# Moving operands in rows of 528 elements and token halves of 256 and 264 in a two-layer hybrid decoder step

## The chip, the cores and the metric

The kernel runs on one core of a Trainium2 chip. The metric is the time of one execution on the device in microseconds (us); lower is better. Times of runs are given as the median of several executions; where a profile is read, it is one execution taken by the hardware profiler.

## The reference: what is computed

One inference step of a decoder with two layers, for a prompt of 512 tokens and 8 sample tokens, 1,024 features wide, all in float32. Layer 0 is a Mamba-2 (SSD) mixer, layer 1 a gated short convolution; each starts with an RMS norm and ends with a residual add, and a last RMS norm follows. Cut to what matters here:

```python
h = rmsnorm(x, norm_w[0])
proj = h @ w_in                         # 1024 -> 5152: z (2048), x/B/C (3072), dt (32)
xBC = silu(causal_dwconv(xBC) + conv_b)
y, state = ssd_chunked(xs, dt, A, B, C, ssm_state)
y = grouped_rmsnorm((y + D * xs) * silu(z), norm_w, 4)
x = x + y @ w_out                       # 2048 -> 1024

h = rmsnorm(x, norm_w[1])
bg, cg, xin, z = split(h @ sc_w_in)     # 1024 -> 4 x 2048
x = x + (bg * causal_dwconv(cg * xin) * silu(z)) @ sc_w_out
y = rmsnorm(x, final_norm_w)
```

Nearly all of the arithmetic is in the four products with weight matrices: `ssd_w_in`, `ssd_w_out`, `sc_w_in`, `sc_w_out`.

## The kernel before, in words

Activations lie transposed in SBUF: features on the 128 partitions, the 520 tokens (512 prompt and 8 sample, `T`) along the free dimension. The 1,024 features of a layer's input are `KT` = 8 rows of 520 tokens (`hhi[:, k, :]`), the 2,048 features that go into an output projection are 16 rows.

**Three products for one.** To keep float32 accuracy at the rate of the rounded type fp32r, weights and activations are split into a rounded high part and a low remainder: `whi`, `wlo` for the weights (ScalarE's `high`, L527, rounds a chunk of 128x1024; VectorE's `low`, L1065, subtracts), `hhi`, `hlo` for the inputs, `yhi`, `ylo` for what enters an output projection. A product is then whi·hhi + whi·hlo + wlo·hhi, accumulated in PSUM. The moving operand of each of these matmuls is a part of a row of `hhi`, `hlo`, `yhi` or `ylo`; the weights are the stationary operand, and each matmul record has a weight load record of its own.

**Two halves.** A PSUM bank holds 512 float32 columns, so the 520 tokens are cut into two halves of `TH` = 260, each with a matmul and a bank of its own:

```python
TH = T // 2
...
for k in range(KT):
    for i, (w, h) in enumerate(((whi, hhi), (whi, hlo), (wlo, hhi))):
        for b, cols in ((b0, slice(0, TH)), (b1, slice(TH, T))):
            mm = pe.matmul(b, w[:, slot, k * P:(k + 1) * P], h[:, k, cols],
                           start=(k == 0 and i == 0), stop=(k == KT - 1 and i == 2))
```

This is `project` (matmul at L1818), 48 matmuls for one chunk of weights. `project_first` (L1801, L1805) is the same for the first chunk, `project_dt` (L1757) projects the 32 time steps with 64 weight columns, `out_part` (L1878) and `out_phase` (L2083) are the output projections of layer 0 and layer 1. In layer 0 the two halves of a chunk meet in the middle of a two-bank tensor `pair` (columns 252 to 512 and 512 to 772), so that VectorE can read all 520 as one run; in layer 1 each half starts at the first column of a bank. `group_sums` (L1891) and L2111 sum squares with a matrix of ones in plain float32; VectorE and ScalarE read such banks half by half (L1107, L1110, L1629, L1630, L1656 to L1672, L1692, L1693).

**Order of the work.** Each engine has its own instruction stream, written out by hand, and semaphores between them. SyncE loads weight chunks of 512 KB (`raw`, 2 slots), ScalarE and VectorE split them (4 slots), TensorE consumes them in the same order. Layer 0 is unrolled over four groups of heads (`LAYER0`), and mixes the projections with the scan's small matmuls; it ends near 460 us. Layer 1 is a loop of 16 steps over `block1`, each with four projections (z, cg, xin, bg), then `out_phase`, twice 8 chunks with 4x12 matmuls.

**Where rows lie.** In the compiled program `hhi` begins at byte 33,152 of each partition, `hlo` at 49,792, `yhi` at 124,032 and `ylo` at 132,352, all of them multiples of 128. A row of 520 elements takes 2,080 bytes and a half 1,040, so the 16 halves of a tensor start 0, 16, 32, ... 112 bytes past a multiple of 128, in turn.

Of the kernel before, what the change touches and what calls it, by code (L numbers as in the profile page):

```python
# [23 lines left out]
F32R = mybir.dt.float32r  # L24
# [7 lines left out]
SEQ = 512  # L32
NB = 8
T = SEQ + NB
TH = T // 2
KT = D // P
DI = 2048
HEADS, HD, GROUPS, NS = 32, 64, 4, 128
# [48 lines left out]
def hybrid_step(nc, ins, outs):  # L87
    x_prompt, x_sample = ins["x_prompt"], ins["x_sample"]

    with ExitStack() as ctx:  # L90
# [9 lines left out]


        def half(p, hb):
            return pair[p][:, COL0 + hb * TH:COL0 + (hb + 1) * TH]

        def whole(p):
            return pair[p][:, COL0:COL0 + T]


        xT = sb("xT", [P, KT, T])
        hhi = sb("hhi", [P, KT, T], F32R)  # L110
        hlo = sb("hlo", [P, KT, T], F32R)
        raw = sb("raw", [P, RAW, 1024])
        whi = sb("whi", [P, SLOT, 1024], F32R)
        wlo = sb("wlo", [P, SLOT, 1024], F32R)
        ybuf = sb("ybuf", [P, 2 * STEPS, T])
        yhi = sb("yhi", [P, STEPS, T], F32R)
        ylo = sb("ylo", [P, STEPS, T], F32R)
        ext = sb("ext", [P, 2, EXT1])
        acc = sb("acc", [P, CONV1])
        thx = sb("thx", [P, T])  # L120
# [47 lines left out]
        x_nat = [flat[:, t * D:(t + 1) * D] for t in range(4)] + [zh[0:NB, :, :].rearrange("p a b -> p (a b)")[:, 0:D]]  # L168
        cs_nat = turned[0:NB * PRE0, 0:XBC]
        ss_nat = st[0:NB * PRE1, :, :].rearrange("p a b -> p (a b)")  # L170
        yhf = yhi[:, :, :].rearrange("p a b -> p (a b)")
        x_norm = [sample[:, (2 + i) * D:(3 + i) * D] for i in range(3)] + [sqs[:, :, :].rearrange("p a b -> p (a b)")[:, 0:D]]
        xs_sq, xs_norm, xs_w = thx[0:NB, 0:D // 2], xs[0:NB, :, :].rearrange("p a b -> p (a b)")[:, 0:D], acc[:, 0:KT * NB]
        emf = em[:, :, :].rearrange("p a b -> p (a b)")
# [320 lines left out]
        def _(act):  # L495
# [23 lines left out]
                ex.then_inc(done, 1)  # L519

            def group_parts(g):
                return (sqs[:, g, 0:TH], bank[6][:, 0:TH]), (sqs[:, g, TH:T], bank[7][:, 0:TH])

            def high(n, slot, turn):

# [476 lines left out]


            act.wait_ge(stat_mm, GROUPS + 1)
            parts = (sqs[:, 1, 0:TH], bank[6][:, 0:TH]), (sqs[:, 1, TH:T], bank[7][:, 0:TH])
            logs(parts, D)
            roots(parts, rs_done, GROUPS + 1)

# [40 lines left out]
        def _(dve):  # L1049
# [52 lines left out]
            def dt_bias():  # L1102
                dve.wait_ge(par_in, 112)
                dve.wait_ge(dt_mm, 1)
                halves = (bank[6], slice(0, TH)), (bank[7], slice(TH, T))
                for b, cols in halves:
                    dve.tensor_scalar(dtv[:, cols], b[0:HEADS, 0:TH], hcol[:, 0:1], None, ALU.add).then_inc(dt_sum, 1)  # L1107
                dve.wait_ge(dt_sum, 2)
                for b, cols in halves:
                    dve.tensor_tensor(dtv[:, cols], dtv[:, cols], b[HEADS:2 * HEADS, 0:TH], ALU.add).then_inc(dt_v, 1)  # L1110
                dve.wait_ge(dt_s, 1)
                dve.tensor_scalar(hcol[:, 3:4], hcol[:, 2:3], -1.0, None, ALU.mult).then_inc(dt_v, 1)

# [508 lines left out]
            def residual(base, half, i):  # L1622
                if i < 3:
                    dve.wait_ge(out_mm, 3 * half + i + 1)
                else:
                    dve.wait_ge(proj_done, base + 8 * (half + 1))
                k = 4 * half + i
                dve.wait_ge(h_hi, 2 * KT)
                dve.tensor_tensor(xT[:, k, 0:TH], xT[:, k, 0:TH], bank[2 * i][:, 0:TH], ALU.add)  # L1629
                dve.tensor_tensor(xT[:, k, TH:T], xT[:, k, TH:T], bank[2 * i + 1][:, 0:TH], ALU.add).then_inc(out_evac, 1)  # L1630


            r1, r2 = sqs[:, 1, :], sqs[:, 2, :]
# [13 lines left out]
            def block1(J, side, ahead=0):  # L1647
                for jj in range(2):
# [5 lines left out]

                    dve.wait_ge(proj_done, j * 4 + (IN1 + 1))
                    dve.tensor_tensor(zr[:, 0:TH], bank[0][:, 0:TH], r1[:, 0:TH], ALU.mult)  # L1656
                    dve.tensor_tensor(zr[:, TH:T], bank[1][:, 0:TH], r1[:, TH:T], ALU.mult).then_inc(z_free, 1)
                    low(j * 4 + (IN1 + SLOT), 0)

                    dve.wait_ge(proj_done, j * 4 + (IN1 + 2))  # L1660
                    dve.tensor_tensor(u[:, 0:TH], bank[2][:, 0:TH], r2[:, 0:TH], ALU.mult).then_inc(u_done, 1)
                    dve.tensor_tensor(u[:, TH:T], bank[3][:, 0:TH], r2[:, TH:T], ALU.mult).then_inc(cg_free, 1)
                    dve.tensor_copy(dec[:, :, 0:PRE1], cst1[:, ds(j, 1), :, :].squeeze(1)).then_inc(cs1_done, 1)
                    low(j * 4 + (IN1 + 1 + SLOT), 1)

# [6 lines left out]
                    dve.tensor_tensor(dec[:, :, PRE1], bank[5][:, SEQ - TH:TH], u[:, SEQ:T], ALU.mult).then_inc(xin_free, 1)  # L1672
# [20 lines left out]
                    dve.tensor_tensor(yt[:, TH:T], bank[7][:, 0:TH], c2[:, TH:T], ALU.mult).then_inc(bg_free, 1)  # L1693
                    low(j * 4 + (IN1 + 3 + SLOT), 3)

            with dve.Fori(0, STEPS) as J:
# [18 lines left out]
        def _(pe):  # L1715
# [34 lines left out]
            def project_dt():  # L1750
                pe.wait_ge(dtw_hi, 1)
                pe.wait_ge(dtw_lo, 1)
                pe.wait_ge(h_lo, KT)
                for k in range(KT):
                    for i, h in enumerate((hhi, hlo)):
                        for half in range(2):
                            mm = pe.matmul(bank[6 + half][0:2 * HEADS, 0:TH], dws[:, k, :], h[:, k, half * TH:(half + 1) * TH],  # L1757
                                           start=(k == 0 and i == 0), stop=(k == KT - 1 and i == 1))
                mm.then_inc(dt_mm, 1)

# [103 lines left out]
            def out_part(g, what, part):  # L1864
                if (g, what) not in NUMBER:
                    return
                n = NUMBER[g, what]
                slot = n % SLOT
                p, turn = PAIR[g, what, part]
                pe.wait_ge(hi_done, n + (SLOT + 1))  # L1870
                pe.wait_ge(lo_done, n + (SLOT + 1))
                pair_empty(p, turn)
                for k in range(STEPS):
                    pe.wait_ge(yg_hi, (g - 1) * STEPS + k + 1)
                    pe.wait_ge(yg_lo, (g - 1) * STEPS + k + 1)
                    for i, (w, y) in enumerate(((whi, yhi), (whi, ylo), (wlo, yhi))):
                        for hb in range(2):
                            mm = pe.matmul(half(p, hb),  # L1878
                                           w[:, slot, k * 256 + part * P:k * 256 + (part + 1) * P],
                                           y[:, k, hb * TH:(hb + 1) * TH],  # L1880
                                           start=(k == 0 and i == 0), stop=(k == STEPS - 1 and i == 2))
                mm.then_inc(proj_done if part else half_done, 1)

            def group_sums(g):
                if g not in PASSES:
                    return
                pe.wait_ge(sqs_done, STEPS * (g + 1) + 1)
                pe.wait_ge(yd_done, 8 * (g + 1) + 1)
                pe.wait_ge(yo_done, STEPS * (g + 1) + 1)
                for half in range(2):  # L1890
                    mm = pe.matmul(bank[6 + half][:, 0:TH], ones[:, :], sqs[:, g, half * TH:(half + 1) * TH], start=True, stop=True)  # L1891
                mm.then_inc(stat_mm, 1)

            def turn_B(g):
# [169 lines left out]
            def out_phase(base):  # L2064

                with pe.Fori(0, 2) as half:
                    for c in range(8):
# [4 lines left out]
                        for i in range(4):  # L2072
# [6 lines left out]
                            for kk in range(2):  # L2079
                                yh, yl = y_slot(2 * c + kk)  # L2080
                                for v, (w, y) in enumerate(((whi, yh), (whi, yl), (wlo, yh))):
                                    for hb in range(2):
                                        mm = pe.matmul(bank[2 * i + hb][:, 0:TH],  # L2083
                                                       w[:, c % SLOT, kk * 512 + i * P:kk * 512 + (i + 1) * P],
                                                       y[:, hb * TH:(hb + 1) * TH],
                                                       start=(c == 0 and kk == 0 and v == 0),
                                                       stop=(c == 7 and kk == 1 and v == 2))
                            if c == 7 and i < 3:
# [3 lines left out]
            def block1(j, first=False):  # L2092
                def part(m, h_ready=None):
                    if first and m < 2:
                        pe.wait_ge(res_add, ADDED[GROUPS, "o3", m] + 1)
                    if first and m == 2:
                        pe.wait_ge(xd_done, TILES)
                        pe.wait_ge(tail_c, 1)
                    project(j * 4 + (IN1 + m), m, bank[2 * m][:, 0:TH], bank[2 * m + 1][:, 0:TH], h_ready)
                pe.wait_ge(z_free, j + 1)  # L2100
                part(0, KT if first else None)
                pe.wait_ge(cg_free, j + 1)
# [3 lines left out]
                if first:  # L2106

                    pe.wait_ge(xsum_done, 7)
                    pe.wait_ge(ln_done, GROUPS)
                    for half in range(2):  # L2110
                        mm = pe.matmul(bank[6 + half][:, 0:TH], ones[:, :], sqs[:, 0, half * TH:(half + 1) * TH], start=True, stop=True)  # L2111
# [66 lines left out]
```

## Time and profile before

| | |
|---|---|
| time, median of 3 runs | 926.89 us (925.6 to 929.68) |
| profiled execution, first to last instruction (span) | 925.8 us |
| profiled execution's own time outside that span | not given apart from the runs; the median is 1.1 us above the span |
| TensorE (PE) busy | 885.2 us (96%), 7,385 matmuls |
| VectorE (DVE) busy | 627.2 us (68%) |
| ScalarE (ACT) busy | 405.6 us (44%) |
| GpSimd (POOL) busy | 142.9 us (15%) |
| mean granted clock of TensorE | 0.993 |

A matmul's own duration in the profile contains the way through the array and overlaps its successor; what a matmul costs in a dense stream is the distance between the starts of two of them. The timeline merges the two halves of one product into one row (x2), so the distance of two such rows is the cost of a pair of halves.

### The profile page before, as it was taken

How to read it: one execution, taken by the hardware profiler on the slowest of the kernel's cores; microseconds unless marked ns; L12 is line 12 of the kernel's file. 1: busy time of each engine (PE TensorE's matmuls, PEld its weight loads, DVE VectorE, ACT ScalarE, POOL GpSimd, SP SyncE). 2: the span in 40 equal slices, each digit the busy share in tenths (PEclk: the TensorE clock that was granted, in tenths of full speed). 3: DMA queues.
4: the chain of work that ended last, by engine and by line, in shares of the span. 5: the costliest groups of instructions: out<-in, count | busy, mean ns of one | idle time of the engine just before them, and what ended most of it. 6: DMA issues, size and time to landing. Idle time of an engine off the chain costs nothing.

```text
span 925.8 us, 19336 instructions
## 1 busy us (share of the span) xinstructions
PE 885.2 (96%) x7385; PEld 870.9 (94%) x7385; DVE 627.2 (68%) x1039; ACT 405.6 (44%) x757; POOL 142.9 (15%) x95
## 2 busy tenths in 40 slices
PE   5999899899989999979999999999999999999996
PEld 5899889899989998968999999999999999999996
DVE  4579999979997899987555555555555555564543
ACT  6556857545864576744432222222222222243343
POOL 5303531243143312450000000000000000000000
PEclk9989999999999999999999999999999999999999
DMA  7427636563475437723333333333333333222212
GB/s 170 115 69 208 181 86 196 167 156 104 138 210 158 133 105 218 199 74 92 92 91 114 91 91 91 91 91 91 91 91 91 91 91 91 91 88 94 92 45 93
DMA packets 162993, 108.00 MB, mean 117 GB/s; under 512 B 5000, under 2 KB 155152, under 8 KB 162368
## 3 DMA queue, kind: packets, MB, share of 16 engines
q1 hardware_dynamic: 123876, 76.15, 28.4%
q10 hardware_dynamic: 38756, 30.61, 11.5%
q0 software_dynamic: 304, 0.48, 0.3%
q8 instruction: 35, 0.57, 0.3%
q14 instruction: 22, 0.18, 0.1%
HBM read 95.35 MB, written 12.14 MB: 116 GB/s over the span
## 4 chain that ended last, share of the span: by engine, by line
PE 53%; DVE 2%; issue 1%; ACT 1%; POOLq 0%; POOL 0%; DVEq 0%; ACTq 0%
PE pair L1818 20%; PE bank L1818 19%; PE pair L2083 5%; PE bank L2083 5%; PE pair L1878 3%; DVE ybuf L1710 0%; PE bank L1891 0%; POOLq L90 0%; ACT sqb L818 0%; DVE acc L1680 0%; ACT xT L976 0%; DVE sqs L1398 0%; DVE ylo L1645 0%; PE bank L2148 0%; DVE yr L1370 0%
## 5 line engine op out<-in xcount | busy, mean ns | idle before, releaser
L527 ACT ACTIVATE whi<-raw 128x1024 fp32r<-128x1024 f32 x136 | 143.6, 1058 | 338.2 <-PE bank L1818 136.8
L1818 PE MATMUL pair<-hhi,whi 128*128 128x260 f32 x1136 | 232.4, 286 | 0.3 <-DVE acc L1195 0.3
L1818 PE MATMUL pair<-hhi,wlo 128*128 128x260 f32 x1136 | 229.6, 284 | 0.0
L1818 PE MATMUL pair<-hlo,whi 128*128 128x260 f32 x1136 | 229.1, 283 | 0.0
L1065 DVE TENSOR_TENSOR wlo<-raw,whi 128x1024 fp32r<-128x1024 f32 x132 | 184.2, 1396 | 22.7 <-ACT whi L527 20.6
L1818 PEld LDWEIGHTS pair<-hhi,whi 128*128 128x128 f32 x1136 | 176.0, 190 | 2.8 <-DVE acc L1195 1.7
L1818 PEld LDWEIGHTS pair<-hlo,whi 128*128 128x128 f32 x1136 | 175.9, 189 | 0.0
L1818 PEld LDWEIGHTS pair<-hhi,wlo 128*128 128x128 f32 x1136 | 175.9, 189 | 0.0
L1818 PE MATMUL bank<-hhi,whi 128*128 128x260 f32 x512 | 103.1, 282 | 0.9 <-ACT sqs L512 0.9
L1818 PE MATMUL bank<-hhi,wlo 128*128 128x260 f32 x512 | 103.2, 283 | 0.0
L1818 PE MATMUL bank<-hlo,whi 128*128 128x260 f32 x512 | 103.0, 283 | 0.0
L1818 PEld LDWEIGHTS bank<-hhi,whi 128*128 128x128 f32 x512 | 78.9, 188 | 1.3 <-ACT sqs L512 1.3
L1818 PEld LDWEIGHTS bank<-hhi,wlo 128*128 128x128 f32 x512 | 78.9, 188 | 0.0
L1818 PEld LDWEIGHTS bank<-hlo,whi 128*128 128x128 f32 x512 | 78.7, 188 | 0.0
L1878 PE MATMUL pair<-yhi,whi 128*128 128x260 f32 x256 | 53.6, 290 | 10.6 <-issue 8.7
L442 POOL TENSOR_TENSOR sample<-sample 128x1024 f32<-128x1024 f32 x16 | 45.1, 2821 | 107.8 <-DVE sample L1363 98.5
L1195 DVE SCALAR_TENSOR_TENSOR acc<-pair,colA,acc 128x512 f32<-128x512 f32 (+1 forms) x72 | 54.1, 751 | 5.1 <-ACT acc L654 3.3
L1878 PEld LDWEIGHTS pair<-yhi,whi 128*128 128x128 f32 x256 | 39.7, 190 | 12.9 <-issue 11.9
L1878 PE MATMUL pair<-ylo,whi 128*128 128x260 f32 x256 | 51.6, 283 | 0.0
L1878 PE MATMUL pair<-yhi,wlo 128*128 128x260 f32 x256 | 51.5, 283 | 0.0
L783 ACT ACTIVATE sample<-sample,dcch 128x128 f32<-128x128 f32 x128 | 39.1, 389 | 10.8 <-DMA out_new_ssm_s<-sample 7.0
L711 ACT ACTIVATE em<-abc,acol 128x128 f32<-128x128 f32 x128 | 39.1, 391 | 2.0 <-issue 2.0
(256 smaller groups left out, 1303.6 us busy)
## 6 DMA issues: line engine op xcount, KB each, us to landing
raw<-in_sc_w_in SPq DMA_DIRECT2D x64, 512.0 KB, 4.0
raw<-in_ssd_w_in SPq DMA_DIRECT2D x40, 512.0 KB, 4.0
abc<-a_rows ACTq DMA_DIRECT2D x16, 512.0 KB, 4.7
sample<-in_state_ssm ACTq DMA_DIRECT2D x16, 512.0 KB, 7.9
out_new_ssm_s<-sample ACTq DMA_DIRECT2D x16, 512.0 KB, 4.3
raw<-in_ssd_w_out SPq DMA_DIRECT2D x16, 512.0 KB, 3.9
raw<-in_sc_w_out SPq DMA_DIRECT2D x16, 512.0 KB, 3.5
sample<-bc_rows ACTq DMA_DIRECT2D x4, 1024.0 KB, 6.8
```

Source lines behind the costliest of these rows:

```text
L442: pool.tensor_tensor(tdec, st[:, q % 2, :].rearrange("p (b n) -> p b n", n=NS), bcbc[:, :, 1, :], ALU.mult).then_inc(t2_done, 1)
L527: act.activation(whi[:, slot, :], raw[:, slot % RAW, :], ACT.Copy).then_inc(hi_done, 1)
L711: e = act.activation(em[:, h, c * Q:(c + 1) * Q], abc[:, h, c * Q:(c + 1) * Q], ACT.Relu, scale=-1.0, bias=acol[:, c, 2 * i + h:2 * i + h ...
L783: d = act.activation(s, s, ACT.Copy, scale=dcf[:, i * NB + b:i * NB + b + 1])
L1065: dve.tensor_tensor(wlo[:, slot, :], raw[:, slot % RAW, :], whi[:, slot, :].bitcast(F32), ALU.subtract).then_inc(lo_done, 1)
L1195: t = dve.scalar_tensor_tensor(acc[:, 0:n], pair[p][:, COL0 - PRE0 + k:COL0 - PRE0 + k + n], cw0(k, tile), acc[:, 0:n], ALU.mult, ALU.add)
L1818: mm = pe.matmul(b, w[:, slot, k * P:(k + 1) * P], h[:, k, cols], start=(k == 0 and i == 0), stop=(k == KT - 1 and i == 2))
L1878: mm = pe.matmul(half(p, hb), w[:, slot, k * 256 + part * P:k * 256 + (part + 1) * P], y[:, k, hb * TH:(hb + 1) * TH], start=(k == 0 and i ...
L2083: mm = pe.matmul(bank[2 * i + hb][:, 0:TH], w[:, c % SLOT, kk * 512 + i * P:kk * 512 + (i + 1) * P], y[:, hb * TH:(hb + 1) * TH], start=(c ...
```

## The change

Rows of `hhi`, `hlo`, `yhi` and `ylo` are allocated with 528 elements (2,112 bytes) of which the first 520 are used; each of these four tensors grows by 8 elements a row. The first half becomes 256 tokens and the second 264, so a half starts 0 or 1,024 bytes into its row. Every place that reads or writes a half takes its new width, and the first half in `pair` now starts at column 256. The order and the number of instructions are the same on all engines; only sizes and addresses differ. In the compiled program the four tensors still begin at multiples of 128 bytes (33,152, 50,048, 124,544, 132,992), so halves of rows with even k start at a multiple of 128 bytes, and those of odd k 64 bytes past one.

```diff
-TH = T // 2
+TH = 256
+TR = T - TH
+ROW = 528
...
         def half(p, hb):
-            return pair[p][:, COL0 + hb * TH:COL0 + (hb + 1) * TH]
+            return pair[p][:, 512:512 + TR] if hb else pair[p][:, COL0:512]
...
-        hhi = sb("hhi", [P, KT, T], F32R)
-        hlo = sb("hlo", [P, KT, T], F32R)
+        hhi_rows = sb("hhi_rows", [P, KT, ROW], F32R)
+        hhi = hhi_rows[:, :, 0:T]
+        hlo_rows = sb("hlo_rows", [P, KT, ROW], F32R)
+        hlo = hlo_rows[:, :, 0:T]
...
-        yhi = sb("yhi", [P, STEPS, T], F32R)
-        ylo = sb("ylo", [P, STEPS, T], F32R)
+        yhi_rows = sb("yhi_rows", [P, STEPS, ROW], F32R)
+        yhi = yhi_rows[:, :, 0:T]
+        ylo_rows = sb("ylo_rows", [P, STEPS, ROW], F32R)
+        ylo = ylo_rows[:, :, 0:T]
...
-                dve.tensor_tensor(xT[:, k, TH:T], xT[:, k, TH:T], bank[2 * i + 1][:, 0:TH], ALU.add).then_inc(out_evac, 1)
+                dve.tensor_tensor(xT[:, k, TH:T], xT[:, k, TH:T], bank[2 * i + 1][:, 0:TR], ALU.add).then_inc(out_evac, 1)
...
-                                           y[:, k, hb * TH:(hb + 1) * TH],
+                                           y[:, k, hb * TH:TH + hb * TR],
...
-                                        mm = pe.matmul(bank[2 * i + hb][:, 0:TH],
+                                        mm = pe.matmul(bank[2 * i + hb][:, 0:TR if hb else TH],
                                                        w[:, c % SLOT, kk * 512 + i * P:kk * 512 + (i + 1) * P],
-                                                       y[:, hb * TH:(hb + 1) * TH],
+                                                       y[:, hb * TH:TH + hb * TR],
...
-                    project(j * 4 + (IN1 + m), m, bank[2 * m][:, 0:TH], bank[2 * m + 1][:, 0:TH], h_ready)
+                    project(j * 4 + (IN1 + m), m, bank[2 * m][:, 0:TH], bank[2 * m + 1][:, 0:TR], h_ready)
```

## Rows read from the trace of the kernel before

**Rows 1.** The page's first part, busy time of each engine over the whole execution:

```profile
PE 885.2 (96%) x7385; PEld 870.9 (94%) x7385; DVE 627.2 (68%) x1039; ACT 405.6 (44%) x757; POOL 142.9 (15%) x95
```

**Rows 2.** Chain of waits in order of time: start us, length us, what:

```profile
508.01 11.53 PE bank L1818 x96
...
840.63 2.88 PE bank L2083 x24
```

**Rows 3.** Longest waits: who waited for whom, us in total, times, longest:

```profile
ACT whi L527 <- PE bank L1818: 136.8, 30, 4.8
...
DVE zh L1656 <- PE pair L1818: 48.3, 14, 3.4
```

**Rows 4.** Busy time by stretch: us, then engines' busy us, clock, DMA share, GB/s:

```profile
250.00:300.00 50.00, 47.57 (x413) 46.81 (x413) 44.70 (x73) 27.77 (x64) 17.64 (x9) 1.00 0.63 186
...
600.00:650.00 50.00, 50.00 (x419) 50.00 (x418) 26.07 (x49) 10.62 (x11) 0.00 (x0) 1.00 0.30 87
```

**Rows 5.** Groups of TensorE's instructions by shape: count, busy us, mean ns:

```profile
L1818 PE MATMUL pair<-hhi,whi 128*128 128x260 f32 x1136 | 232.4, 286 | 0.3 <-DVE acc L1195 0.3
...
L1818 PE MATMUL bank<-hhi,whi 128*128 128x260 f32 x512 | 103.1, 282 | 0.9 <-ACT sqs L512 0.9
...
L1878 PE MATMUL pair<-ylo,whi 128*128 128x260 f32 x256 | 51.6, 283 | 0.0
L2083 PE MATMUL pair<-hhi,whi 128*128 128x260 f32 x96 | 19.4, 283 | 0.0
...
L2083 PE MATMUL pair<-yhi,whi 128*128 128x260 f32 x32 | 6.5, 285 | 0.6 <-DVE ylo L1645 0.6
```

**Rows 6.** Timeline of TensorE: first pair of k = 0-4, 7, then next projection:

```profile
600.12 0.40 PE L1818 MATMUL bank<-hhi,whi 128*128 128x260 f32 x2
...
600.83 0.40 PE L1818 MATMUL bank<-hhi,whi 128*128 128x260 f32 x2
...
601.55 0.40 PE L1818 MATMUL bank<-hhi,whi 128*128 128x260 f32 x2
...
602.27 0.41 PE L1818 MATMUL bank<-hhi,whi 128*128 128x260 f32 x2
...
603.01 0.40 PE L1818 MATMUL bank<-hhi,whi 128*128 128x260 f32 x2
...
605.17 0.40 PE L1818 MATMUL bank<-hhi,whi 128*128 128x260 f32 x2
...
605.88 0.40 PE L1818 MATMUL bank<-hhi,whi 128*128 128x260 f32 x2
```

**Rows 7.** Timeline of TensorE near 49 us, and that stretch's row by stretches:

```profile
48.50 0.64 PE L1818 MATMUL pair<-hhi,wlo 128*128 128x260 f32 x2
48.93 0.64 PE L1818 MATMUL pair<-hhi,whi 128*128 128x260 f32 x2
...
45.00:52.00 7.00, 7.00 (x29) 5.84 (x28) 5.26 (x13) 6.93 (x18) 0.00 (x0) 0.51 0.11 29
```

**Rows 8.** The matmuls with 64 weight columns, L1757: durations min/median/max, and timeline:

```profile
L1757 PEld LDWEIGHTS bank<-hhi,yhi x16: 134/134/136, 25.9 to 29.4; 128*64 128x64 f32 x16
...
27.46 0.40 PE L1757 MATMUL bank<-hhi,yhi 128*64 128x260 f32 x2
27.70 0.40 PE L1757 MATMUL bank<-hlo,yhi 128*64 128x260 f32 x2
```

**Rows 9.** Plain float32 matmuls, 260 and 128 columns: timeline, and durations min/median/max:

```profile
465.44 1.04 PE L2111 MATMUL bank<-sqs,ones 128*128 128x260 f32 x4
...
68.11 0.94 PE L1956 MATMUL bank<-xdd,turned 128*128 128x128 f32 x7
...
L2111 PE MATMUL bank<-sqs,ones x4: 381/382/383, 465.4 to 466.1; 128*128 128x260 f32 x4
...
L1956 PE MATMUL bank<-xdd,turned x128: 271/275/377, 68.1 to 388.1; 128*128 128x128 f32 x128
```

More of the change, by code:

```diff
@@ L170, in hybrid_step @@
         ss_nat = st[0:NB * PRE1, :, :].rearrange("p a b -> p (a b)")
-        yhf = yhi[:, :, :].rearrange("p a b -> p (a b)")
+        yhf = yhi_rows[:, :, :].rearrange("p a b -> p (a b)")
         x_norm = [sample[:, (2 + i) * D:(3 + i) * D] for i in range(3)] + [sqs[:, :, :].rearrange("p a b -> p (a b)")[:, 0:D]]
@@ L521, in group_parts @@
             def group_parts(g):
-                return (sqs[:, g, 0:TH], bank[6][:, 0:TH]), (sqs[:, g, TH:T], bank[7][:, 0:TH])
+                return (sqs[:, g, 0:TH], bank[6][:, 0:TH]), (sqs[:, g, TH:T], bank[7][:, 0:TR])
             def high(n, slot, turn):
@@ L1004, in _ @@
             act.wait_ge(stat_mm, GROUPS + 1)
-            parts = (sqs[:, 1, 0:TH], bank[6][:, 0:TH]), (sqs[:, 1, TH:T], bank[7][:, 0:TH])
+            parts = (sqs[:, 1, 0:TH], bank[6][:, 0:TH]), (sqs[:, 1, TH:T], bank[7][:, 0:TR])
             logs(parts, D)
@@ L1106, in dt_bias @@
                 for b, cols in halves:
-                    dve.tensor_scalar(dtv[:, cols], b[0:HEADS, 0:TH], hcol[:, 0:1], None, ALU.add).then_inc(dt_sum, 1)
+                    dve.tensor_scalar(dtv[:, cols], b[0:HEADS, 0:cols.stop - cols.start], hcol[:, 0:1], None, ALU.add).then_inc(dt_sum, 1)
                 dve.wait_ge(dt_sum, 2)
                 for b, cols in halves:
-                    dve.tensor_tensor(dtv[:, cols], dtv[:, cols], b[HEADS:2 * HEADS, 0:TH], ALU.add).then_inc(dt_v, 1)
+                    dve.tensor_tensor(dtv[:, cols], dtv[:, cols], b[HEADS:2 * HEADS, 0:cols.stop - cols.start], ALU.add).then_inc(dt_v, 1)
                 dve.wait_ge(dt_s, 1)
@@ L1656, in block1 @@
                     dve.tensor_tensor(zr[:, 0:TH], bank[0][:, 0:TH], r1[:, 0:TH], ALU.mult)
-                    dve.tensor_tensor(zr[:, TH:T], bank[1][:, 0:TH], r1[:, TH:T], ALU.mult).then_inc(z_free, 1)
+                    dve.tensor_tensor(zr[:, TH:T], bank[1][:, 0:TR], r1[:, TH:T], ALU.mult).then_inc(z_free, 1)
                     low(j * 4 + (IN1 + SLOT), 0)
@@ L1661, in block1 @@
                     dve.tensor_tensor(u[:, 0:TH], bank[2][:, 0:TH], r2[:, 0:TH], ALU.mult).then_inc(u_done, 1)
-                    dve.tensor_tensor(u[:, TH:T], bank[3][:, 0:TH], r2[:, TH:T], ALU.mult).then_inc(cg_free, 1)
+                    dve.tensor_tensor(u[:, TH:T], bank[3][:, 0:TR], r2[:, TH:T], ALU.mult).then_inc(cg_free, 1)
                     dve.tensor_copy(dec[:, :, 0:PRE1], cst1[:, ds(j, 1), :, :].squeeze(1)).then_inc(cs1_done, 1)
@@ L1671, in block1 @@
                     dve.tensor_tensor(row[:, PRE1 + TH:PRE1 + SEQ], bank[5][:, 0:SEQ - TH], u[:, TH:SEQ], ALU.mult)
-                    dve.tensor_tensor(dec[:, :, PRE1], bank[5][:, SEQ - TH:TH], u[:, SEQ:T], ALU.mult).then_inc(xin_free, 1)
+                    dve.tensor_tensor(dec[:, :, PRE1], bank[5][:, SEQ - TH:TR], u[:, SEQ:T], ALU.mult).then_inc(xin_free, 1)
                     dve.wait_ge(xin_free, j + 2)
@@ L1692, in block1 @@
                     dve.tensor_tensor(yt[:, 0:TH], bank[6][:, 0:TH], c2[:, 0:TH], ALU.mult)
-                    dve.tensor_tensor(yt[:, TH:T], bank[7][:, 0:TH], c2[:, TH:T], ALU.mult).then_inc(bg_free, 1)
+                    dve.tensor_tensor(yt[:, TH:T], bank[7][:, 0:TR], c2[:, TH:T], ALU.mult).then_inc(bg_free, 1)
                     low(j * 4 + (IN1 + 3 + SLOT), 3)
@@ L1755, in project_dt @@
                     for i, h in enumerate((hhi, hlo)):
-                        for half in range(2):
-                            mm = pe.matmul(bank[6 + half][0:2 * HEADS, 0:TH], dws[:, k, :], h[:, k, half * TH:(half + 1) * TH],
+                        for b, cols in ((bank[6], slice(0, TH)), (bank[7], slice(TH, T))):
+                            mm = pe.matmul(b[0:2 * HEADS, 0:cols.stop - cols.start], dws[:, k, :], h[:, k, cols],
                                            start=(k == 0 and i == 0), stop=(k == KT - 1 and i == 1))
@@ L1890, in group_sums @@
                 for half in range(2):
-                    mm = pe.matmul(bank[6 + half][:, 0:TH], ones[:, :], sqs[:, g, half * TH:(half + 1) * TH], start=True, stop=True)
+                    mm = pe.matmul(bank[6 + half][:, 0:TR if half else TH], ones[:, :], sqs[:, g, half * TH:TH + half * TR], start=True, stop=True)
                 mm.then_inc(stat_mm, 1)
@@ L2110, in block1 @@
                     for half in range(2):
-                        mm = pe.matmul(bank[6 + half][:, 0:TH], ones[:, :], sqs[:, 0, half * TH:(half + 1) * TH], start=True, stop=True)
+                        mm = pe.matmul(bank[6 + half][:, 0:TR if half else TH], ones[:, :], sqs[:, 0, half * TH:TH + half * TR], start=True, stop=True)
                     mm.then_inc(stat_mm, 1)
```

## The prediction

> **What bounds the kernel now.** I read the busy times first. TensorE is busy for 885.2 of 925.8 us and the next engine, VectorE, for 627.2 [rows 1]. A busy share does not say who waits for whom, so the chain of waits comes next: in layer 1 it is nothing but matmuls, piece after piece of 96 at L1818 in 11.53 us, and 24 at L2083 in 2.88 us [rows 2]. The waits say the same from the other side: ScalarE's rounding of weights and VectorE's first multiply of a step wait for TensorE, 136.8 and 48.3 us in total [rows 3]. The stretches show how much room there is. At 600 us TensorE is full and VectorE half idle; at 250 us TensorE is at 47.57 of 50 us and VectorE at 44.70 [rows 4]. So in layer 1 a nanosecond more or less per matmul is a nanosecond of the kernel; in layer 0 VectorE would take over as the bound after a few per cent.
>
> **What one matmul costs.** 11.53 us over 48 pairs of halves is 240.2 ns a pair, 120.1 a matmul; at L2083 it is 2.88 over 12 pairs, 240.0 [rows 2]. The stretch from 45 to 52 us, with a granted clock of 0.51, that is 1.2 GHz for nearly all of it, has pairs 0.43 us apart [rows 7]: 217 ns for 260 columns, or 0.83 ns a column. That is one column per cycle and nothing besides. At 2.4 GHz the same 260 columns are 108.3 ns, and the stream shows 120.1. The missing **11.8 ns** are the only thing the change can act on, so I ask what they are.
>
> Not the array: plain float32 matmuls of 260 columns (L2111) start (1.04 - 0.382) / 3 = 0.219 us apart [rows 9], two cycles for each column plus 2.5 ns. Not the weight load: at L1757 only 64 weight columns are loaded, the load's record falls to 134 ns, and the pairs are still 0.24 us apart [rows 8]. It is something that shows only when a 4-byte column is wanted every cycle of the fast clock: how the moving row is delivered. That is what the change touches.
>
> **Is it the place where a half starts?** The trace of before answers this in part. Every tensor starts at a multiple of 128 bytes, and halves start 0, 16, ... 112 bytes past one. In rows with even k the first half starts on a multiple of 64 bytes, in rows with odd k neither half does. If a start off such a boundary cost something, even k would be shorter. The starts of k are 600.12, 600.83, 601.55, 602.27, 603.01 [rows 6]: 0.71 and 0.72 us for even k, 0.72 and 0.74 for odd, and 0.71 for k = 7. Three halves of an even k start on a 64-byte boundary, so the difference of at most 0.02 us would be 7 ns for each, but k = 7 beside k = 0 shows none. The whole projection is 5.76 us for 8 k's. I take no gain from the starts.
>
> **Part by part.** The matmuls with fp32r operands number 3 x (1,136 + 512 + 256) + 6 x (96 + 32) = 6,480 at L1818, L1878 and L2083 [rows 5] (each of these rows stands three times, those of L2083 six), and 80 more in the first projections: 6,560, or 3,280 pairs of one half each, 788 us in all. Before, a pair is 260 + 260 columns; after, 256 + 264. *First half, 256 columns:* no row has it. Its lower bound is 111 ns: float32 matmuls of 128 columns at two cycles each, with the same 128 weight columns to load, start (0.94 - 0.275) / 6 = 0.111 us apart [rows 9], and 256 columns at full clock are 106.7. Its upper bound is today's 120.1. *Second half, 264 columns:* at least 110 ns of columns, 112.5 with the 2.5 ns of L2111; above, I allow one more step of 7 to 13 ns, 127 to 133. Between ends so far apart I take the value that the nearest row gives, the 260 columns themselves, with the 11.8 ns as a fixed cost of an instruction and 0.417 ns a column: 118.4 and 121.8, again **240.2 a pair. The sum of this term is 0.** The float32 sums of squares have 520 columns a pair before and after: 0. VectorE and ScalarE read 256 + 264 where they read 260 + 260, 0.0 together, and they wait for TensorE in layer 1 [rows 3]; in layer 0 VectorE's sum per chunk stays too, so even without cover it is 0. The longer rows move no DMA and add no instruction. Nothing is reordered; no wait is added.
>
> The profiled execution spans 925.8 us, 1.1 below the median of the runs. With a sum of 0 the forecast is the median, **926.9 us**.
>
> **The rivals.**
>
> *A. The row is delivered in whole blocks (faster).* 120.0 ns is also what nine blocks of 128 bytes would take at full clock (288 columns), and a half of 1,040 bytes meets nine such blocks at every one of its eight starts. So the evenness in [rows 6], which I used against starts, does not speak against blocks: they would give just this flat picture. After the change a first half of 1,024 bytes meets 8 blocks in even rows and 9 in odd ones, a second half always 9. A quarter of the matmuls would fall to the 111 ns of [rows 9]: 1,640 x 9 = 15 us. With blocks of 64 bytes (17 now, 16 and 17 after, 7.06 ns each) it is 3,280 x 7.1 = 23 us; with blocks of 32 columns counted from the start of the matmul, 3,280 x 9 = 30 us. Layer 1 has 64 x 24 + 384 = 1,920 of the 3,280 pairs and passes it on in full; of layer 0's 41% I count half, since VectorE is nearly full there [rows 4]. That leaves 12 to 24 us: 903 to 915, middle 908. For it speaks the odd coincidence with 288; against it, that a fixed cost gives 120 as well, without needing a last block to be paid in full.
>
> *B. The excess goes altogether (much faster).* If a row starting and ending well costs only its columns, a pair falls to 111 + 112.5 = 223.5: 16.7 x 3,280 = 55 us, 44 after the discount: 883. Against it: first halves of even k already start on a boundary and save nothing visible. The Trainium skill, "TensorE: Matmul & The Clock Gate", section "Back-to-back issue gap", puts the distance of two matmuls at the full clock at N / 2.4 + 2.5 ns. For 260 columns that is 110.8 where this trace shows 120.1, so the page does not describe the stream before; were it right for aligned rows, it would be this rival, at 221.7 ns a pair as an estimate from the page.
>
> *C. A floor that 264 leaves (slower).* Suppose that 120 ns is a floor per matmul that does not depend on the columns up to 260, for weights and moving row together. Then 256 gains nothing, and 264 costs more by 4 columns, 1.7 ns, or by a further block, 7.1 ns: 5 to 23 us, 932 to 950, middle 940. It decides from the point at which the second half starts a successor more than 1.4 ns later than now while the first stays. Against it: with half the weight columns the distance is the same 0.24 us [rows 8], and small matmuls would need another floor, since L1956 runs at 111.
>
> *D. The change doesn't do what it says:* odd rows lie 64 bytes past a 128-byte multiple, so if 128 is what counts, half of the rows stay off it. That is within A's lower price.
>
> **How the numbers follow.** Fixed cost, no change: 0.52. A: 0.27. B: 0.09. C: 0.12. About 0.5%, 4.6 us, is what a measurement of this kernel can tell from no change. A and B lie beyond it on the fast side, 0.36; a little of the no-change case may fall there too, and as much of C falls back into it: faster 0.37, same 0.52, slower 0.11. The range reaches over A, whose own middle is 908, down to 900, and to the low end of C, 933; left out are B, A's last few us and most of C, 0.2 together. Within no change alone the range would be 924 to 930.
>
> **What would show it.** With fixed cost, the pieces of 96 matmuls stay at 11.53 us, and first halves start their successor 3 to 4 ns sooner than second halves. Under A the piece falls to 11.1 to 11.3 us, under 128-byte blocks with even k shorter than odd by some 27 ns, and ScalarE's wait for L1818 shrinks by the same sum. Under B it falls to 10.7. Under C it grows to 11.6 or more. I am wrong if a piece differs from 11.53 by more than 0.06 us; and if the pieces stay but the time moves, my account of layer 0 is wrong instead.

## The result, and the profile after

The changed kernel takes 932.68 us (median of 13 runs, 930.67 to 934.78) against 927.99 for the kernel before (13 runs, 925.51 to 931.59). The ratio is 1.0049, with a 95% interval of 1.0036 to 1.0063: slower by 4.7 us, clear of the noise, where the sum of the prediction was 0.

The profiled execution of the changed kernel spans 931.5 us. The first part of its page, in the order of [rows 1]:

```profile
PE 892.9 (96%) x7385; PEld 878.8 (94%) x7385; DVE 626.4 (67%) x1039; ACT 405.6 (44%) x757; POOL 142.8 (15%) x95
```

TensorE is busy for 7.7 us longer than in [rows 1] with the same number of instructions; no other engine moves by more than 0.8. The time is in the matmuls themselves. The chain of waits in order of time (start us, length us, what) says in which; the projection that was L1818 is L1824 here, the output phase L2089:

```profile
450.43 11.65 PE pair L1824 x96
...
510.70 11.65 PE bank L1824 x96
...
826.08 3.15 PE pair L2089 x24
...
840.69 2.84 PE bank L2089 x24
...
846.44 2.93 PE bank L2089 x24
```

The two lines of the kernel before between which layer 1's input projections lie:

```profile
448.30 11.54 PE pair L1818 x96
...
820.21 3.14 PE pair L2083 x24
```

Beside [rows 2], a piece of 96 matmuls in layer 1's input projections has grown from 11.53 to 11.65 us: a pair of halves from 240.2 to 242.7 ns. From the first of these pieces to the first of the output phase the chain has 375.7 us where before it had 371.9: **3.7 us** of the 4.7. The output phase, from its first matmul's start to its last one's end, takes 92.3 us and took 92.4. Its pieces of 24 do change, from 2.87 to 2.90 us before to anything between 2.84 and 2.93, but they come to the same sum.

The timeline of TensorE, first pair of each k of one projection, as in [rows 6]:

```profile
603.77 0.40 PE L1824 MATMUL bank<-hhi_rows,whi 128*128 128x256 f32 x2
...
604.50 0.41 PE L1824 MATMUL bank<-hhi_rows,whi 128*128 128x256 f32 x2
...
605.22 0.40 PE L1824 MATMUL bank<-hhi_rows,whi 128*128 128x256 f32 x2
...
605.95 0.41 PE L1824 MATMUL bank<-hhi_rows,whi 128*128 128x256 f32 x2
...
606.68 0.40 PE L1824 MATMUL bank<-hhi_rows,whi 128*128 128x256 f32 x2
```

A k now takes 0.73, 0.72, 0.73 and 0.73 us, where [rows 6] have 0.71, 0.72, 0.72 and 0.74. No k is short, as blocks of 128 bytes would have made the even ones; nearly all are a little long.

Layer 1's first projection starts 2.1 us later in this profile (450.43 against 448.30 in the two chains). Here the two profiled executions differ in something else. A stretch of the changed kernel's run, and the same one before (us, engines' busy us, granted clock, DMA share, GB/s), changed kernel first:

```profile
98.20:101.60 3.40, 3.40 (x20) 3.08 (x17) 3.35 (x7) 1.93 (x3) 2.46 (x1) 0.50 0.44 129
```

```profile
98.20:101.60 3.40, 3.40 (x35) 3.23 (x32) 3.36 (x7) 2.26 (x4) 2.07 (x1) 1.00 0.33 101
```

The changed kernel's profile has two stretches at 1.2 GHz that the profile before does not have, this one and one from 166.40 to 169.80 us: 20 matmuls where there were 35, and 18 where there were 31. TensorE had been idle 0.57 and 2.02 us, waiting for VectorE, shortly before the first of them:

```profile
94.69 0.66 PE L1726 MATMUL bank<-ident,xs 128*128 128x128 f32 x4 [0.57 <-DVE xs L1223]
97.36 1.24 PE L1977 MATMUL bank<-em,xd 128*64 128x128 f32 x16 [2.02 <-DVE em L1295]
```

I take that for chance rather than layout. Executions of the kernel before have mean granted clocks from 0.982 to 0.993, and their times follow: those at 0.993 take 924.7 to 927.5 us, those at 0.984 and below 930.0 to 932.0. At one clock the layouts still differ: at 0.991 and 0.992 the kernel before takes 925.0 to 927.7 us, the changed kernel 930.7 to 931.9. So the 2.1 us of layer 0 in this one profile are not to be read as the change's; over many runs layer 0 is left with 4.7 - 3.7 = 1.0 us. Its matmuls are dearer too: where they follow each other without a wait at full clock, the starts in the two traces are on average 120.7 ns apart against 119.8 at L1824 (L1818 before) and 120.5 against 119.8 at L1884 (L1878 before).

The waits, as in [rows 3], show the slower stream as its consumers see it:

```profile
ACT whi L533 <- PE bank L1824: 138.8, 30, 4.8
```

136.8 before, 138.8 now: ScalarE merely waits longer.

### The profile page after: what moved, and what is told of

The parts are those of the page before. It is cut to its first block, busy times and chain, and to the rows that moved or that the text cites. A ratio compares the mean times of both kernels' runs of the same rounds, so it can differ in the third digit from the quotient of the medians.

```text
span 931.5 us, 19336 instructions
## 1 busy us (share of the span) xinstructions
PE 892.9 (96%) x7385; PEld 878.8 (94%) x7385; DVE 626.4 (67%) x1039; ACT 405.6 (44%) x757; POOL 142.8 (15%) x95
## 4 chain that ended last, share of the span: by engine, by line
PE 53%; DVE 2%; issue 1%; ACT 1%; POOLq 0%; POOL 0%; DVEq 0%; ACTq 0%
PE pair L1824 20%; PE bank L1824 19%; PE pair L2089 5%; PE bank L2089 5%; PE pair L1884 3%; DVE ybuf L1716 0%; PE bank L1897 0%; POOLq L92 0%; ACT sqb L824 0%; DVE acc L1686 0%; ACT xT L982 0%; DVE sqs L1404 0%; DVE ylo_rows L1651 0%; PE bank L2154 0%; DVE yr L1376 0%
## 5 line engine op out<-in xcount | busy, mean ns | idle before, releaser
L533 ACT ACTIVATE whi<-raw 128x1024 fp32r<-128x1024 f32 x136 | 143.6, 1058 | 339.8 <-PE bank L1824 138.8
L1824 PE MATMUL pair<-hhi_rows,whi 128*128 128x256 f32 x1136 | 233.8, 287 | 0.0
L1824 PE MATMUL pair<-hhi_rows,wlo 128*128 128x256 f32 x1136 | 231.5, 286 | 0.0
L1824 PE MATMUL pair<-hlo_rows,whi 128*128 128x256 f32 x1136 | 230.4, 285 | 0.0
L1824 PEld LDWEIGHTS pair<-hhi_rows,whi 128*128 128x128 f32 x1136 | 178.7, 191 | 2.7 <-issue 2.7
L1824 PEld LDWEIGHTS pair<-hlo_rows,whi 128*128 128x128 f32 x1136 | 177.7, 190 | 0.0
L1824 PEld LDWEIGHTS pair<-hhi_rows,wlo 128*128 128x128 f32 x1136 | 176.9, 189 | 0.0
L1824 PE MATMUL bank<-hhi_rows,whi 128*128 128x256 f32 (+1 forms) x512 | 104.0, 284 | 0.9 <-ACT sqs L518 0.9
L1824 PE MATMUL bank<-hhi_rows,wlo 128*128 128x256 f32 (+1 forms) x512 | 104.2, 285 | 0.0
L1824 PE MATMUL bank<-hlo_rows,whi 128*128 128x256 f32 (+1 forms) x512 | 103.3, 283 | 0.0
L1824 PEld LDWEIGHTS bank<-hhi_rows,whi 128*128 128x128 f32 x512 | 80.2, 190 | 1.4 <-ACT sqs L518 1.4
L1824 PEld LDWEIGHTS bank<-hlo_rows,whi 128*128 128x128 f32 x512 | 79.6, 189 | 0.0
L1824 PEld LDWEIGHTS bank<-hhi_rows,wlo 128*128 128x128 f32 x512 | 79.1, 188 | 0.0
L1884 PE MATMUL pair<-yhi_rows,whi 128*128 128x256 f32 (+1 forms) x256 | 54.1, 293 | 9.7 <-issue 7.8
L1884 PE MATMUL pair<-ylo_rows,whi 128*128 128x256 f32 (+1 forms) x256 | 52.6, 288 | 0.0
L1884 PE MATMUL pair<-yhi_rows,wlo 128*128 128x256 f32 (+1 forms) x256 | 52.5, 287 | 0.0
L1884 PEld LDWEIGHTS pair<-yhi_rows,whi 128*128 128x128 f32 x256 | 40.5, 192 | 12.1 <-issue 11.3
L1884 PEld LDWEIGHTS pair<-yhi_rows,wlo 128*128 128x128 f32 x256 | 40.6, 193 | 0.0
```

What stands on the lines that cost most here:

```text
L533: act.activation(whi[:, slot, :], raw[:, slot % RAW, :], ACT.Copy).then_inc(hi_done, 1)
L1884: mm = pe.matmul(half(p, hb), w[:, slot, k * 256 + part * P:k * 256 + (part + 1) * P], y[:, k, hb * TH:TH + hb * TR], start=(k == 0 and i ...
```

## The experiments

I compare pieces of 96 matmuls, since they repeat within 0.01 us in an execution once layer 1 has got going, and take whole times where a version is worth having. Where distances of single matmuls are given, they are means over 60 to 63 of the 64 projections of layer 1, worked out from the start times in the trace. Ratios are to the kernel before in the same session; e3, e4, e7, e8, e10, e11 and e12 ran once, and the pieces are what is read of them.

**Is it the split or the rows?** Two kernels take the change apart. The first, e1, keeps rows of 520 elements:

```diff
-ROW = 528
+ROW = 520
```

> Halves of 256 and 264, rows kept at 520 elements. In layer 1 the changed kernel has pieces of 96 matmuls at L1824 of 11.65 us against 11.53 before. Theory P (place): what costs is where the halves lie, now all on multiples of 64 bytes, with a picture that repeats every 4 rows. Then rows of 520 spread the starts again and the piece falls back to about 11.53 us, the time to within 1 us of before. Theory W (width): the uneven split costs, because 256 columns do not get cheaper than about 120 ns. Then the piece stays at 11.65 and the time 5 to 6 us above before.

The second, e2, keeps halves of 260:

```diff
-TH = 256
+TH = 260
```

> Rows of 528 elements, halves kept at 260 and 260. Theory P: the second halves start 16 bytes past a multiple of 64, first halves on one, so part of the cost stays: piece of 96 between 11.53 and 11.65 us, time 0 to 6 us above before. Theory W: piece 11.53, time as before.

Chain of waits of the first, then of the second:

```profile
507.10 11.53 PE bank L1824 x96
```

```profile
508.46 11.52 PE bank L1824 x96
```

Times: 927.73 us against 928.07, ratio 1.0003 (0.9990 to 1.0016), and 927.24, ratio 0.9985 (0.9969 to 1.0001). **Neither half of the change costs anything; only both together do.** Theory W, the width, is out: with rows of 520 a first half of 256 takes 118.4 ns and a second of 264 takes 122.0, as the prediction had it (118.4 and 121.8). The second kernel came out slightly below the span that theory P gave it. What sets the changed kernel apart from these two is that every half starts on a multiple of 64 bytes.

**Is the weight load in it?** Layer 1's projections with 64 of the 128 weight columns, once on the changed kernel (e3) and once on the kernel before (e7); half of layer 1's outputs are left out.

```diff
-                            mm = pe.matmul(b, w[:, slot, k * P:(k + 1) * P], h[:, k, cols],
+                            mm = pe.matmul(b[0:wide, :], w[:, slot, k * P:k * P + wide], h[:, k, cols],
```

> The changed kernel, but in layer 1's input projections only 64 of the 128 weight columns are loaded and multiplied (half of the outputs of layer 1 are left out). Theory L (the weight load's reads and the moving row's reads meet in SBUF): the piece of 96 falls from 11.65 us to at most 11.4, and the spread from place to place (116 to 127 ns) shrinks. Theory P without the load: piece stays at 11.65 us, with the same picture per row.

> The kernel before, with 64 instead of 128 weight columns in layer 1's input projections (half of layer 1's outputs left out). The same edit on the changed kernel took its piece of 96 from 11.65 to 11.41 us. If the whole difference between the two layouts comes from moving row and weight load meeting (theory L), halving the load brings both to nearly the same, 11.41 here too, at least 11.35 to 11.45 (from 11.53). If the layouts differ by the moving rows alone (theory A), the difference of 0.12 us stays: 11.29 or, if the load costs nothing in this layout, 11.53.

Changed kernel's layout, then the layout before:

```profile
508.27 11.41 PE bank L1824 x96
```

```profile
504.40 11.40 PE bank L1818 x96
```

The 0.12 us between the layouts shrinks to 0.01 when the weight load is halved. The moving row alone does not tell the layouts apart; row and load together do. The spread from place to place shrank little: 115 to 124 ns, where the changed kernel has 116 to 128. And 118.8 ns a matmul remain in both, so halving the load takes away only a small part of the 11.8 ns; what the other half of the load costs no run shows.

**Which places?** Moving operands 16 bytes on (e5; all four tensors), then weights 16 bytes on and `wlo` 48 (e6), then weights 64 bytes on (e8), each from the changed kernel.

```diff
-        hhi = hhi_rows[:, :, 0:T]
+        hhi = hhi_rows[:, :, 4:4 + T]
...
-        yhi = yhi_rows[:, :, 0:T]
+        yhi = yhi_rows[:, :, 4:4 + T]
```

> The changed kernel with all moving operands 16 bytes further on (elements 4 to 524 of each row of 528), so that every half starts 16 bytes past a multiple of 64; the weights stay on multiples of 64. Theory A (a half that starts on a multiple of 64 bytes is itself dear when its predecessor ended there too): piece of 96 matmuls back from 11.65 to about 11.53 us, time 5 us less than the changed kernel. Theory L (what counts is how the weight load's addresses lie to the moving row's): also back to about 11.53, since the two are no longer in step. Theory B (neither; only that rows step by 2,112 bytes and halves by 1,024): piece stays at 11.65.

```diff
-        whi = sb("whi", [P, SLOT, 1024], F32R)
-        wlo = sb("wlo", [P, SLOT, 1024], F32R)
+        whi_room = sb("whi_room", [P, SLOT * 1024 + 8], F32R)
+        whi = whi_room[:, 4:4 + SLOT * 1024].rearrange("p (s n) -> p s n", n=1024)
+        wlo_room = sb("wlo_room", [P, SLOT * 1024 + 8], F32R)
+        wlo = wlo_room[:, 4:4 + SLOT * 1024].rearrange("p (s n) -> p s n", n=1024)
```

> The changed kernel with whi 16 bytes further on and wlo 48, the moving operands unchanged on multiples of 64. Theory A: piece stays at 11.65 us, time as the changed kernel's. Theory L: the piece falls back to about 11.53. Theory B: stays at 11.65.

```diff
+        gap_w = sb("gap_w", [P, 16])
         raw = sb("raw", [P, RAW, 1024])
```

> The changed kernel with raw, whi, wlo and all that follows 64 bytes further on; hhi and hlo unchanged. Theory L with places counted over more than 64 bytes: the piece moves away from 11.65 us by 0.03 or more, in either direction, and the picture of the distances per row changes. Theory A: piece and picture as in the changed kernel.

Chain of waits of the three, in this order:

```profile
509.11 11.44 PE bank L1824 x96
```

```profile
507.11 11.52 PE bank L1826 x96
```

```profile
509.56 11.65 PE bank L1825 x96
```

Moving the moving operands takes the piece to 11.44, below the kernel before, where no theory had put it (11.53 or 11.65): 923.39 us against 926.66, ratio 0.9967 (0.9950 to 0.9985). Moving the weights, with no operand of layer 1's projections moved besides, takes it to 11.52, which theory A excludes: 928.1 against 926.66, ratio 1.0021 (1.0006 to 1.0037), against the changed kernel's 1.0049. Moving the weights by 64 bytes leaves the piece at 11.65; theory L with a longer period had asked for a change of the piece or of the picture, and the picture did change. Here are the distances of the six matmuls of a k, in ns (whi·hhi, whi·hlo, wlo·hhi, two halves each):

```
changed kernel   k=0  116.7 123.3 119.2 121.7 127.5 120.8
                 k=1  125.0 120.8 117.5 117.5 117.5 120.8
                 k=2  116.7 122.5 125.0 125.8 115.8 125.0
                 k=3  126.7 119.2 117.5 122.5 122.5 125.8
weights +64      k=0  126.7 119.2 117.5 122.5 122.5 125.8
                 k=1  116.7 123.3 119.2 121.7 127.5 120.8
                 k=2  125.0 120.9 117.5 117.5 117.5 120.8
                 k=3  116.7 122.5 125.0 125.8 115.8 125.0
```

**The picture has moved down by one row of k, to a tenth of a nanosecond.** A row of the moving operand lies 2,112 bytes after the last, 64 more than a multiple of 256, and the weights of a k lie 512 bytes after the last, a multiple of 256. Weights 64 bytes on therefore have the same effect as a moving operand one row back. So in the steady stream, for steps of 64 bytes, the distances follow *moving start less weights start, modulo 256 bytes*, and neither address alone decides them. Whether that holds for steps of 16 bytes as well is not shown: in e6 the third product's difference takes the values it has in e5, one row of k later, but its distances are not those of e5 (117.2 and 120.0 ns in row 1, 113.6 and 117.2 in e5's row 0); the matmuls around it have other differences there.

**A wrong extrapolation.** Moving operands 32 bytes on (e9; again all four tensors):

```diff
-        hhi = hhi_rows[:, :, 0:T]
+        hhi = hhi_rows[:, :, 8:8 + T]
```

> The changed kernel with all moving operands 32 bytes further on (elements 8 to 528 of each row). Under theory L the cost of a matmul is a function of its moving row's start less its weights' start, taken modulo 64: 0 gives 121.4 ns a matmul (the changed kernel), 16 gives 119.2 (moving operands 16 bytes on), and a mix of two thirds 48 and one third 16 gives 120.0, so 48 alone about 120.4. The mean of the four is the 120.1 of the kernel before, so 32 should give 119.4 to 119.8: piece of 96 matmuls 11.46 to 11.50 us, time 1 to 3 us below before. Theory A (only a start on a multiple of 64 is dear): 11.44 as with 16.

```profile
505.80 11.52 PE bank L1824 x96
```

11.52, above the 11.46 to 11.50 that the sum had given; the time is 926.91 against 928.32, ratio 0.9987 (0.9968 to 1.0005). In the projections the order is 0 dear, 16 cheap, 32 between, but the four values modulo 64 do not average to the kernel before: there the two halves of a pair have different differences, and what stands before and behind a matmul may matter. In the output phase the order is another one: the same matmuls are on average 119.9 ns apart with 0, 119.5 with 16 and 120.2 with 32.

**The same difference in every row.** From the kernel with 16 bytes, in e10 all eight k of layer 1's projections read row 0 (layer 1's inputs other than row 0 are left out of the products):

```diff
-                            mm = pe.matmul(b, w[:, slot, k * P:(k + 1) * P], h[:, k, cols],
+                            mm = pe.matmul(b, w[:, slot, k * P:(k + 1) * P], h[:, 0 if one_row else k, cols],
```

> The kernel with moving operands 16 bytes on, but layer 1's input projections read the row k = 0 for all eight k (layer 1's results are left wrong in value; the number and shape of all instructions stay). Every difference of starts is then the same modulo 256. In the picture of the kernel with 16 bytes the six matmuls of k = 0 mean 117.6 ns, of k = 1 to 3 119.3, 120.2 and 119.5. If the cost goes by the difference modulo 256, the piece of 96 is 11.29 us; if modulo 64 only, it stays at 11.44.

Chain, the first piece and one of the later ones:

```profile
445.45 11.53 PE pair L1824 x96
...
504.39 11.31 PE bank L1824 x96
```

11.31 us where 11.29 was expected. The six distances are the same for every k: 117.5, 123.2, 112.8, 122.4, 113.5, 117.8. The weights moved on by 512 bytes each k and made no difference. By itself this shows that 512 bytes more change nothing; that 256 is enough shows in the table above, where the difference of the starts grows by 6,400 bytes, 25 times 256, in four rows and the picture returns.

**The same places can also cost more.** The first piece of this run takes 11.53 us and not 11.31. The first three projections of layer 1 have the same operands in the same places as the later ones, but settle into 118, 118, 122, 118, 118 and 126 ns, 120.0 on average, again the same for every k. After the wait before the fourth projection, within which TensorE runs the sums of squares, the cheaper picture sets in and stays. The fourth, like the first three, stands outside the loop of steps, so the loop is not what makes it cheap. Nor are the other engines busier in the dear part, but less: VectorE is busy for 6.8 of the 17 us from 445 and for 12.0 of the 17 us from 475, and the DMA share is 0.22 against 0.43. So the differences of the starts do not fix the cost alone. That it goes by how the stream began is the likely reading, but no run tests it.

**What are the 11.8 ns?** Three kernels vary the width: second halves of 256 (e4), then 260 columns (e11) in layer 1's projections (8 and 4 of the sample tokens of layer 1 are left out), and halves of 128 and 392 everywhere (e12). The edits:

```diff
-                    project(j * 4 + (IN1 + m), m, bank[2 * m][:, 0:TH], bank[2 * m + 1][:, 0:TR], h_ready)
+                    project(j * 4 + (IN1 + m), m, bank[2 * m][:, 0:TH], bank[2 * m + 1][:, 0:TR - 8], h_ready, T - 8)
```

> The changed kernel, but in layer 1's input projections the second half is 256 columns too (the 8 sample tokens of layer 1 are left out). Fixed cost per instruction with 0.417 ns a column: 8 columns less in every second matmul, 3.3 ns, so the piece of 96 falls by 0.16 us to 11.49. Delivery in whole blocks of 64 bytes or more: falls by 48 x 7 ns = 0.34 us or more. A floor of 120 ns: falls by at most 0.1 us.

```diff
-                    project(j * 4 + (IN1 + m), m, bank[2 * m][:, 0:TH], bank[2 * m + 1][:, 0:TR], h_ready)
+                    project(j * 4 + (IN1 + m), m, bank[2 * m][:, 0:TH], bank[2 * m + 1][:, 0:TR - 4], h_ready, T - 4)
```

> The changed kernel with second halves of 260 columns in layer 1's input projections (4 of 8 sample tokens of layer 1 left out). 264 gave a piece of 96 of 11.65 us, 256 gave 11.23. Cost by columns alone: half way, 11.44. Whole blocks of 64 bytes: 260 costs what 264 does, 11.65. A step at 256, with a small price a column: near 11.57.

```diff
-TH = 256
+TH = 128
```

> The changed kernel with halves of 128 and 392 columns (rows of 528, all starts on multiples of 64 bytes). It asks whether the 11 to 12 ns that 260 columns take beyond 108.3 are a fixed cost of an instruction or grow with the columns. Fixed: 392 columns take 163.3 + 11.8 = 175 ns. In proportion (0.462 ns a column): 181 ns. The 128 columns are bound by the load of their successor's 128 weight columns, 111 ns or a little more if that load is slowed too. So a pair is 286 ns if the cost is fixed, 292 if proportional, against 242.8 in the changed kernel: piece of 96 matmuls 13.7 or 14.0 us, and a time of about 1,065 to 1,090 us.

Chains, in this order:

```profile
508.10 11.23 PE bank L1824 x96
```

```profile
509.06 11.39 PE bank L1824 x96
```

```profile
565.55 13.92 PE bank L1824 x96
```

With a first half of 256 and everything on multiples of 64 bytes, a pair costs 234.0 ns with a second half of 256, 237.3 with 260 and 242.7 with 264: 3.3 ns for four columns and 5.4 for the next four, where four columns at full clock are 1.7. The fall of 0.42 us in e4 was what whole blocks had forecast, but e11 excludes them, since 260 lies clear of 264, though 1,040 and 1,056 bytes need equally many blocks of 64; excluded too is a floor of 120 ns, since two halves of 256 take 117.0 each; and a fixed cost with 0.417 ns a column holds for rows of 520 but not here. Halves of 128 and 392 take 290 ns a pair (13.92 / 48) and 1,067.9 us in all, between the two forecasts of 286 and 292. How a pair divides cannot be read from the matmuls: their starts in the trace are 58 and 232 ns apart in turn, so that the one of 392 starts long before the 111 ns that the forecast gave the 128. The starts of the weight loads are 108 and 182 ns apart. By the loads, the 392 columns cost about 182, in proportion (181); by the 111 to 112 ns of [rows 9] for the 128, they cost 178, between fixed (175) and in proportion. The run does not decide. **What the greater part of the 11.8 ns is stays open.**

## Why the prediction was right or wrong

*What bounds the kernel:* right. The distance of matmuls is what moved, and it went through layer 1 in full: 3.7 us of 4.7, where 2.5 ns a pair on 1,536 pairs are 3.8.

*No gain from the starts:* right in what it excluded, wrong in what it concluded. The starts in [rows 6] compared even k with odd k within one layout, in which each k of eight has another difference to the weights. That tells about places on average over all sixteen residues; it could not tell what a layout does in which all halves sit on the same one modulo 64. And the rows were read too mildly: over 60 projections of the trace k = 3 takes 741 ns and k = 7 takes 710, so the 0.74 us of k = 3 was a real effect of place.

*"The fixed cost of an instruction and 0.417 ns a column: 118.4 and 121.8, again 240.2 a pair. The sum of this term is 0":* **this is the step that failed.** With rows of 520 it is right to 0.2 ns (118.4 and 122.0). With rows of 528 the pair measures 242.7 in layer 1's projections: first halves take 120.6 ns, second halves 122.0. The term is +2.5 ns a pair on 1,536 pairs there, 3.8 us, and not 0. I priced the width and the place each by itself, and each by itself is indeed free; I had no term for the two together. It fails by the prediction's own signs too: the piece was to stay within 0.06 us of 11.53 and moved by 0.12, and first halves were to be 3 to 4 ns shorter than second halves and are 1.4 shorter.

*"Not the weight load":* too quick. The timeline in [rows 8] shows the distance with 64 weight columns as 0.24 us a pair to two digits; the single starts of these matmuls in the same trace are 119.2 ns apart on average. In layer 1's projections (e3, e7) it is 118.8 to 118.9 ns against 120.1 before and 121.4 in the changed kernel. Halving the load is worth 1.3 and 2.5 ns, and the whole difference of the two kernels is in that part. A row rounded to 10 ns cannot exclude an effect of 1 ns on 6,560 instructions.

*The rivals:* A, whole blocks, is refuted by e11, and by the changed kernel itself, in which halves of 1,024 bytes are not cheap. B fell with it: rows that start well, by its own definition, cost more. C had the right sign and, in its lower price of 5 us, nearly the right size; the piece of 11.65 us is the sign that the prediction gave for it (11.6 or more). But its mechanism, a floor, is refuted by e4 and e1. D does not apply.

*Range and chances:* 932.7 lies inside 900 to 933, at the very end of it, and 4.7 us is on the line between "same" and "slower" that the prediction drew at 4.6. The forecast of 926.9 stood on three runs of the kernel before; over 13 it takes 927.99, which is 1.1 of the 5.8 us between forecast and result. That the time fell inside is luck: the range reached up there for C, whose mechanism is wrong, and the reasoning that gave no change misses a real cost.

The account for the 4.7 us is thus: 3.7 in layer 1's projections, tied by e1, e2, e5, e6 and e8 to where the halves lie relative to the weights, and by e3 and e7 to the weight load. The remaining 1.0 fits the 0.7 to 0.9 ns that layer 0's 2,720 matmuls are dearer (some 2.3 us, an estimate, of which VectorE's near-full stretches may hide a part), but was not isolated. The output phase has all starts on multiples of 64 bytes too and gains on some rows what it loses on others, 118 ns a matmul in the pieces of 2.84 us and 122 in those of 2.93. Why its sum is spared is open: its differences per row are the same four, its order of rows and weights is another. So "all starts on multiples of 64 bytes" is not dear in every stream.

Two places of the Trainium skill speak of the two streams. "TensorE: Matmul & The Clock Gate", section "Step-by-step: what each phase is for", gives TensorE two independent read ports and says that loading the next tile's weights takes no read bandwidth from the running matmul. "SBUF — State Buffer", section "Who interferes with whom", says that TensorE never waits on anyone; that is said of other engines, and no run here tests it. For a moving stream of 4-byte columns at the full clock the two streams are not free of each other here: with the row where it was, the same matmuls take 121.4 or 120.0 ns according to where the weights lie (e6), and with half the weight columns the two layouts no longer differ. Whether it is read bandwidth that they share is not shown.

## What to carry to other kernels

When TensorE is full and streams fp32r rows at the full clock, where the moving rows lie relative to the weights is a knob worth trying, and it costs no instruction: here `hhi_rows[:, :, 4:4 + T]` instead of `0:T` made the changed kernel 0.8% faster (by the two ratios to the kernel before, 0.9967 and 1.0049) and beat the kernel before (923.39 us against 926.66, interval 0.9950 to 0.9985). Aligning everything to the same boundary is no safe default: here it was the dearest of the layouts tried. Try several offsets on the chip rather than reckon with a rule: each of mine held only for part of the kernel. Before calling an effect absent, count the instructions that it would touch and see whether the row that you read has digits enough: 1 ns was 6.6 us here.

## What the runs showed of the hardware that was not expected

- In layer 1's projections the distance of two fp32r matmuls changes with the moving row's start less the weights' start. Means over a piece were 119.2 (16 bytes, all rows), 120.0 (32), and 121.4 ns (0, modulo 64 each); with the difference at 16 modulo 256 throughout, 117.8 ns (11.31 us for 96). The output phase of the same kernels has 119.5, 120.2 and 119.9, and the same operands in the same places took 120.0 instead of 117.8 in the first three projections of e10.
- A layout with rows of 2,304 bytes, used from 16 bytes on, would have the difference 16 everywhere and was not tried; it needs some 4.6 KB more in each partition (24 rows of 192 bytes). In layer 1's projections alone it would be worth up to (11.53 - 11.31) x 32 = 7 us, an estimate from these pieces that supposes the cheaper of the two pictures.
- In the stretch at 1.2 GHz of [rows 7] the same matmuls are 216.7 ns apart, a cycle a column, and in the changed kernel's stretches at 1.2 GHz they take 213.4 (256 columns) and 220.4 (264): the excess and its dependence on the place were seen at 2.4 GHz only.
- Single distances within a projection range from 112 to 133 ns over the layouts tried and repeat from projection to projection, with a spread of about half a nanosecond.
